# A decoder layer on eight cores: the squares of a 24-tick prologue put last in their ticks, weight loads at other ticks, and eight tile ticks spread over the first own block

## The chip, the cores and the metric

The kernel runs on all 8 cores of one Trainium2 chip, each core on its own 2048 of the 16384 tokens. The metric is device microseconds of the slowest core; the median over runs counts. The engines are PE (TensorE), DVE (VectorE), ACT (ScalarE), POOL (GpSimd) and SP (SyncE, which only issues transfers). Each engine works through its own list of instructions in order, and waits on semaphores.

## What is computed

One decoder layer. The part that matters here is its beginning:

```python
h = rms_norm(x, g_pre_mix[l])
proj = h @ w_in[l]                       # q, k, v (768 each), u (256), gates (2048)
q = apply_rope(q); k = apply_rope(k)
for gi, (window, dilation) in enumerate(((128, 1), (512, 4), (2048, 16))):
    o_g, lse_g = dilated_window_attention(q[group], k[group], v[group], window, dilation)
```

Then the groups are merged by their softmax denominators, a pooling branch and gates are added, an output projection and norm follow, and a SwiGLU FFN with its own norms ends the layer. Since a query looks back up to 2048 tokens, each core also needs k and v of the 2048 tokens ahead of its own, the halo.

## The kernel before

Each core gets its own tokens `xo` (16 tiles of 128 tokens x 1024, f32, 512 KB each) and the halo `xh` (16 tiles, too). Its stages are the halo ticks (to about 82 us), four own blocks of q, k and u projections (to about 210 us), attention (to about 320 us), gates and output projection, and the FFN to the end.

**One tile's way.** SP loads it into `xst` (or, for own tiles 4 to 7, `hTf`). `t_sq` takes its sum of squares on ACT (L394); for halo tiles `rstd_chain` then makes 1/rms in two small POOL instructions (L341, L343), for own tiles ACT takes a root (L400) and `t_rc` a reciprocal on DVE (L404). `t_xs` scales the tile to bf16 in one of three `xsb` buffers, on ACT (L411) for even tiles and on DVE (L413) for odd ones, which frees the load buffer. `t_tr` transposes it on PE in 8 pieces (L424, two PSUM banks in turn), and DVE copies it out with the gain into `hTs` (halo, L432) or `hT` (own). `t_hc` (ACT, L440) keeps 32 columns of each halo tile in `hTc`, for the groups with smaller windows.

**The halo ticks.** Loop over `s_` from 0 to 23. In tick s the tiles s (square), s-2 (scale), s-3 (transpose), s-4 (`t_hc`) and s-8 (`v_stream`: v of group 2, L538) are worked on, and in ticks 7, 8, 11, 12, 15, 16, 19, 20 a `k_stream` (k of group 2 for four tiles: 8 matmuls of 512 columns, L449). Ten buffers hold halo tiles, so tile i+10 is loaded when tile i has been scaled (tick i+2). SP's list is in order: from tick 12 the own tiles 0 to 3 and the tables of cos and sin come in it, at tick 18 the own tiles 4 to 7 and later 8 to 11. In ticks 16 to 22 `own_tick(0)` works on own tiles 0 to 3 in the same stages.

**A rope unit** (`rope_unit`, `rope_flush`): 8 matmuls (L449), an ACT copy to `qb` (L528); then, one unit later, the rotation matmul (L493), two DVE products `t` and `t2b` with the tables (L501, L503) and a POOL addition into `kT` or `qT` (L518). The POOL addition of a unit so stands on POOL in the tick of the flush.

**Weights** come over POOL (`wload`, L74: f32 in memory, cast to bf16 by the transfer). `wplan` says in which tick: `load_wk(g)` and `load_wq(g)` are two transfers of 256 KB (counted as bf16) each, `load_wv(g)` is one of 512 KB. `wk2` and `wv2` are used by the halo ticks (from ticks 7 and 8), the others in the own blocks. `masks` (512 KB) and `wmix` (4 small ones) are first used in attention.

**Own blocks.** Block b has 12 rope units (n = 0 to 11) on own tiles 4b to 4b+3. Block 0 also has, behind n = 3, two halo k units of group 1 (`k_halo`) and four `v_halo`, and behind n = 5 those of group 0. `own_tick(1)` takes the own tiles 4 to 15 through their stages, 8 calls in block 0 and 7 in block 1; `tick_at` says behind which n. Block 1 needs tiles 4 to 7.

## Time and profile before

| | us |
|---|---|
| median of 3 runs | 996.59 |
| lowest run | 996.31 |
| the profiled execution, whole | 1000.57 |
| span of its slowest core (core 7), which all rows below are of | 999.0 |
| spans of the 8 cores | 989.2 to 999.0 |
| PE busy | 926.5 (93%) |
| DVE, ACT, POOL busy | 394.0, 350.3, 320.1 |

The highest of the three runs (1165.07) was a disturbed one and is not used. PE is busy 93% of the span. In forty slices of the page its digit is 9 nearly everywhere but in the first four or five, and there the digit of the DMA engines is 7 to 9. Busy time of PE is modelled at its ends, and in stretches where the granted clock is half, a matmul takes twice as long and still counts as busy.

### The profile page before, as it was taken

The page shows a single profiled execution, that of the slowest core. Times are in us where ns is not written, and L with a number is a line of the kernel's source. Part 1 is how long each engine was busy: PE and PEld are TensorE (multiplying, and loading weights), DVE is VectorE, ACT ScalarE, POOL GpSimd, SP SyncE. Part 2 cuts the span into 40 slices and gives each one's busy share as a digit, 9 for nine tenths or more (in the row PEclk, how much of TensorE's full clock was granted, in tenths as well). Part 3 has the DMA queues.
Part 4 walks back from the last instruction along what each step waited for, and adds up shares of the span by engine and source line. Part 5 has one row for each costly group of instructions (what it writes and reads, how often), then busy time and mean ns, then how long its engine had stood idle before and what let it go on. Part 6 is the DMA issues. An engine that isn't in the chain of part 4 may idle for free.

```text
span 999.0 us, 15229 instructions; the slowest of 8 cores (989.2 to 999.0 us)
## 1 busy us (share of the span) xinstructions
PE 926.5 (93%) x5532; PEld 462.5 (46%) x5532; DVE 394.0 (39%) x552; ACT 350.3 (35%) x603; POOL 320.1 (32%) x318
## 2 busy tenths in 40 slices
PE   1779899998897999999998999999999999999993
PEld 1455454466664444444454444444444444444441
DVE  2576785558876233323677121111112111211111
ACT  4763763369776222224662111110111111111101
POOL 3446587733400433233565111111322000001231
PEclk9999999999998999999999999999999999999997
DMA  8799310000230452114979666664234444430332
GB/s 225 235 231 257 87 47 22 1 2 2 35 53 8 80 84 43 22 22 90 314 252 184 115 110 117 115 108 87 92 127 114 76 85 66 82 64 1 127 110 80
DMA packets 32874, 99.16 MB, mean 99 GB/s; under 512 B 4256, under 2 KB 4256, under 8 KB 32800
## 3 DMA queue, kind: packets, MB, share of 16 engines
q0 software_dynamic: 15296, 42.05, 25.7%
q1 hardware_dynamic: 17360, 56.11, 16.9%
q8 instruction: 45, 0.74, 0.3%
q14 instruction: 29, 0.24, 0.1%
q10 hardware_dynamic: 144, 0.03, 0.0%
HBM read 123.43 MB, written 16.78 MB: 140 GB/s over the span
## 4 chain that ended last, share of the span: by engine, by line
PE 80%; DMA 6%; ACT 4%; issue 4%; DVE 3%; POOL 2%; SPq 1%; DVEq 0%; ACTq 0%; POOLq 0%
PE ps L1229 15%; PE ps L1195 15%; PE ps L1198 15%; PE ps L449 10%; PE ps L969 6%; PE ps L972 6%; PE ps L538 5%; DMA xst<-xh 2%; DMA xin<-xo 2%; DMA xst<-xo 2%; PE ps L979 1%; PE ps L976 1%; PE ps L826 1%; PE ps L804 1%; POOL x1b L1045 1%
## 5 line engine op out<-in xcount | busy, mean ns | idle before, releaser
L1195 PE MATMUL ps<-hT,wgu 128*128 128x512 bf16 x672 | 158.7, 379 | 0.0
L1198 PE MATMUL ps<-hT,wgu 128*128 128x512 bf16 x672 | 158.7, 379 | 0.0
L1229 PE MATMUL ps<-wdn,ffT 128*128 128x512 bf16 x704 | 152.3, 379 | 1.5 <-DMA wdn<-wdn 1.5
L1210 DVE TENSOR_TENSOR ffT<-ps,sa 128x512 bf16<-128x512 f32 x88 | 60.8, 691 | 222.5 <-PE ps L1198 222.5
L1209 ACT ACTIVATE sa<-ps 128x512 f32<-128x512 f32 x88 | 52.7, 598 | 241.5 <-PE ps L1195 241.5
L1229 PEld LDWEIGHTS ps<-wdn,ffT 128*128 128x128 bf16 x704 | 68.8, 98 | 84.7 <-issue 1.9
L1198 PEld LDWEIGHTS ps<-hT,wgu 128*128 128x128 bf16 x672 | 65.7, 98 | 79.3
L1195 PEld LDWEIGHTS ps<-hT,wgu 128*128 128x128 bf16 x672 | 65.6, 98 | 78.6
L74 POOL DMA_DIRECT2D wgu<-wgu x42 | 22.5, 537 | 236.1 <-PE ps L1198 227.5
L449 PE MATMUL ps<-hT,wqk 128*128 128x512 bf16 x384 | 91.6, 383 | 0.6 <-DVE hT L432 0.6
L1045 POOL TENSOR_TENSOR x1b<-tb,xin 128x1024 f32<-128x1024 f32 x31 | 72.8, 2350 | 55.7 <-DVE tb L1040 29.9
L991 POOL TENSOR_TENSOR mT<-m,m 128x512 bf16<-128x512 f32 x32 | 40.5, 1266 | 144.0 <-DVE m L986 144.0
L359 ACT ACTIVATE junk<-ps 128x1024 bf16<-128x1024 f32 x31 | 31.6, 1018 | 139.1 <-PE ps L1229 131.8
L518 POOL TENSOR_TENSOR kT<-t,t2b 128x512 bf16<-128x512 f32 (+1 forms) x36 | 57.5, 1612 | 42.3 <-DVE t2b L503 36.9
L1040 DVE SCALAR_TENSOR_TENSOR tb<-ps,rsA,gfin 128x1024 f32<-128x1024 f32 x15 | 19.3, 1284 | 130.6 <-POOL rsA L343 130.6
L969 PE MATMUL ps<-hT,wgs 128*128 128x512 bf16 x256 | 62.0, 386 | 0.0
L972 PE MATMUL ps<-hT,wgs 128*128 128x512 bf16 x256 | 60.5, 379 | 0.0
L808 ACT ACTIVATE PT<-ps 128x1024 bf16<-128x1024 f32 x48 | 55.4, 1161 | 11.8 <-PE ps L804 11.2
L985 DVE TENSOR_TENSOR m<-ps,sga 128x512 f32<-128x512 f32 x32 | 22.1, 692 | 94.6 <-PE ps L976 91.2
L528 ACT ACTIVATE qb<-ps 128x512 bf16<-128x512 f32 (+1 forms) x60 | 34.9, 584 | 67.8 <-PE ps L449 61.3
L449 PEld LDWEIGHTS ps<-hT,wqk 128*128 128x128 bf16 x384 | 37.3, 99 | 43.6 <-issue 2.5
L1032 PE MATMUL ps<-wout,mT 128*128 128x512 bf16 x256 | 56.9, 379 | 0.0
(131 smaller groups left out, 1175.7 us busy)
## 6 DMA issues: line engine op xcount, KB each, us to landing
wgu<-wgu POOLq DMA_DIRECT2D x42, 512.0 KB, 6.3
xst<-xh SPq DMA_DIRECT2D x16, 512.0 KB, 16.7
xin<-xo SPq DMA_DIRECT2D x16, 512.0 KB, 5.4
x1s<-x1b SPq DMA_DIRECT2D x16, 512.0 KB, 3.7
xin<-x1s SPq DMA_DIRECT2D x16, 512.0 KB, 4.3
out<-x1b SPq DMA_DIRECT2D x15, 512.0 KB, 2.9
xst<-xo SPq DMA_DIRECT2D x12, 512.0 KB, 10.8
wdn<-wdn POOLq DMA_DIRECT2D x22, 256.0 KB, 7.3
```

What stands on the lines that cost most here:

```text
L449: ev = pe.op(lambda e, k=k: e.matmul(ps[:, bank, 0:n], lhsT=wfn(k), rhs=rhsfn(k), start=(k == 0), stop=(k == 7)), signal=(k == 7))
L518: ev_o = pool.op(lambda e: e.tensor_tensor(out=dst, in0=i0, in1=i1, op=ALU.add), waits=[ev_t1, ev_t2])
L808: ev_e = act.op(lambda e: e.activation(out=PT[k3][:, :, :], in_=ps[:, b0:b0 + 2, :], func=AF.Exp, scale=0.125), waits=[ev, pt_free[k3]])
L969: e1 = pe.op(lambda e, k=k, wb=wb, b1=b1, tok=tok: e.matmul(ps[:, b1, :], lhsT=wgs[wb][:, 0, k, :], rhs=hT[:, k, tok], start=(k == 0), sto ...
L972: e2 = pe.op(lambda e, k=k, wb=wb, b2=b2, tok=tok: e.matmul(ps[:, b2, :], lhsT=wgs[wb][:, 1, k, :], rhs=hT[:, k, tok], start=(k == 0), sto ...
L1032: ev = pe.op(lambda e, k=k, hf=hf, pr_=pr_: e.matmul(ps[:, pr_[0] + hf, :], lhsT=mT[:, k, i * 128:(i + 1) * 128], rhs=wout[:, k, hf * 512: ...
L1045: ev_o = pool.op(lambda e: e.tensor_tensor(out=outbuf[:, :], in0=tb[b][:, :], in1=xres[:, :], op=ALU.add), waits=[ev_t, ev_xres, out_free])
L1195: e1 = pe.op(lambda e, k=k, wbuf=wbuf, ba=ba, tok=tok: e.matmul(ps[:, ba, :], lhsT=wbuf[:, 0, k, :], rhs=hT[:, k, tok], start=(k == 0), st ...
L1198: e2 = pe.op(lambda e, k=k, wbuf=wbuf, bb=bb, tok=tok: e.matmul(ps[:, bb, :], lhsT=wbuf[:, 1, k, :], rhs=hT[:, k, tok], start=(k == 0), st ...
L1209: es = act.op(lambda e, ub=ub, ba=ba: e.activation(out=sa[ub][:, :], in_=ps[:, ba, :], func=AF.Silu), waits=[e1, sa_free[ub]])
L1210: ef = dve.op(lambda e, ub=ub, bb=bb, j=j, b=b: e.tensor_tensor(out=ffT[:, j, b * 512:(b + 1) * 512], in0=ps[:, bb, :], in1=sa[ub][:, :], ...
L1229: ev = pe.op(lambda e, j=j, h2=h2, pr_=pr_, il=il: e.matmul(ps[:, pr_[0] + h2, :], lhsT=ffT[:, j, il * 128:(il + 1) * 128], rhs=wdn[:, j, ...
```

## The change

There are four edits. In the halo ticks the square of tile s, with the two POOL instructions behind it, and the weight loads of the tick move from the head of the tick to its end (ahead of `own_tick(0)`). `wplan` has other ticks: wv2 from 1 to 4, wk1 from 11 to 7, wk0 from 13 to 9, wv1 from 15 to 13, wv0 from 17 to 16; the others stay. `masks` and `wmix` are loaded in block 1 behind n = 5 instead of ahead of block 0. In block 0 the eight calls of `own_tick(1)` come behind n = 1, behind each `k_halo(1, ...)`, behind the second and the fourth `v_halo(1, ...)`, and behind n = 5, 7 and 9, instead of behind n = 1, 3, 4, 5, 6, 7, 8, 9.

```diff
-    wplan = {0: [lambda: load_wk(2)], 1: [lambda: load_wv(2)], 2: [lambda: wload("rotm", rotm[:, :], rotm_d[:, :])],
-             11: [lambda: load_wk(1)], 13: [lambda: load_wk(0)], 15: [lambda: load_wv(1)], 17: [lambda: load_wv(0)],
+    wplan = {0: [lambda: load_wk(2)], 4: [lambda: load_wv(2)], 2: [lambda: wload("rotm", rotm[:, :], rotm_d[:, :])],
+             7: [lambda: load_wk(1)], 9: [lambda: load_wk(0)], 13: [lambda: load_wv(1)], 16: [lambda: load_wv(0)],
              19: [lambda: load_wq(2)], 21: [lambda: load_wq(1)], 23: [lambda: load_wq(0)]}
     for s_ in range(NTH + 8):
-        if s_ < NTH:
-            t_sq(s_)
-        for f in wplan.get(s_, ()):
-            f()
         i = s_ - 2
...
             x_load(NTH + s_ - 14)
+        if s_ < NTH:
+            t_sq(s_)
+        for f in wplan.get(s_, ()):
+            f()
         if 16 <= s_ < 23:
             own_tick(0)
...
-    wload("masks", masks[:, :, :], masks_d[:, :, :])
-    for g in range(4):
-        c, hf = g // 2, g % 2
-        wload("wmix", wmixb[64 * hf:64 * hf + 64, c, 64 * hf:64 * hf + 64], wmix_d[g, :, :], waits=[ev_ms4])
     rope_ev = {}
-    tick_at = {0: (1, 3, 4, 5, 6, 7, 8, 9), 1: (0, 2, 4, 6, 8, 9, 10)}
+    tick_at = {0: (1, 5, 7, 9), 1: (0, 2, 4, 6, 8, 9, 10)}
...
                 for pr in range(2):
                     k_halo(1, pr)
+                    own_tick(1)
                 for r in range(4):
                     v_halo(1, r, "dve")
                     if r == 1:
                         rope_flush()
+                    if r % 2:
+                        own_tick(1)
...
             if b == 1 and n == 5:
                 for c2 in range(2):
                     u_halo(c2)
+                wload("masks", masks[:, :, :], masks_d[:, :, :])
+                for g in range(4):
+                    c, hf = g // 2, g % 2
+                    wload("wmix", wmixb[64 * hf:64 * hf + 64, c, 64 * hf:64 * hf + 64], wmix_d[g, :, :], waits=[ev_ms4])
```

SP's list is the same in both kernels. How the others move is seen at three places. First ACT in ticks 5 to 7, as a piece of the difference (`xst_29` holds tile 4, `xst_30` tile 5, `xst_31` tile 6, `xst_32` tile 7; L394 is a square, L411 a scaling, L440 `t_hc`, L528 the copy of the first `k_stream`):

```order
 L394 ACTIVATE junk_39_81,ssA_49<-xst_30_72 128x1024
+L411 ACTIVATE xsb_36_78<-xst_29_71,rsA_51 128x1024
 L440 ACTIVATE hTc_83<-hTs_82 128x8x32
 L394 ACTIVATE junk_38_80,ssA_49<-xst_31_73 128x1024
-L411 ACTIVATE xsb_36_78<-xst_29_71,rsA_51 128x1024
-L440 ACTIVATE hTc_83<-hTs_82 128x8x32
+L440 ACTIVATE hTc_83<-hTs_82 128x8x32
+L528 ACTIVATE qb_52_94<-ps 128x512
 L394 ACTIVATE junk_39_81,ssA_49<-xst_32_74 128x1024
```

The scaling of tile 4 now stands ahead of the square of tile 6, and the copy of the first `k_stream` ahead of the square of tile 7.

Next POOL in ticks 6 to 8, a piece of the difference (L341 and L343 make 1/rms, L518 is the addition of the first `k_stream`):

```order
+L341 TENSOR_SCALAR msA_50<-ssA_49 128x1
+L343 TENSOR_TENSOR rsA_51<-msA_50,nhalf_52 128x1
+L341 TENSOR_SCALAR msA_50<-ssA_49 128x1
+L343 TENSOR_TENSOR rsA_51<-msA_50,nhalf_52 128x1
+L74 DMA wqk_63<-wk 128x1024 x2
 L518 TENSOR_TENSOR kT_16_58<-t_0_54_96,t2b_56_98 128x4x128
 L341 TENSOR_SCALAR msA_50<-ssA_49 128x1
```

The load of wk1 now stands ahead of the first addition, and the pair for tile 8 behind it, where it stood ahead of it before.

Last PE in the halo units of block 0, a piece of the difference (L538 on `hTc` are `v_halo`, L449 on `hT` own units, on `hTd` halo units of group 0, L424 the transposes of own tiles):

```order
 L538 MATMUL ps<-wvr_64,hTc_83 128x256 x16
 L493 MATMUL ps<-qb_53_95,rotm_44 128x512
+L424 MATMUL ps<-ident_43,xsb_37_79 128x128 x8
 L538 MATMUL ps<-wvr_64,hTc_83 128x256 x16
+L424 MATMUL ps<-ident_43,xsb_35_77 128x128 x8
 L449 MATMUL ps<-hT_55,wqk_63 128x512 x16
 L493 MATMUL ps<-qb_52_94,rotm_44 128x512
-L424 MATMUL ps<-ident_43,xsb_37_79 128x128 x8
+L424 MATMUL ps<-ident_43,xsb_36_78 128x128 x8
 L449 MATMUL ps<-hTd_84,wqk_63 128x128 x8
```

Where one own tile had been transposed before the units of group 0, three are now; all of block 0's transposes keep their number, five.

## Rows read from the trace of the kernel before

**Rows 1.** Windows of core 7 by stage; columns as its first line says.
```profile
core 7: us, PE busy (x) PEld busy (x) DVE busy (x) ACT busy (x) POOL busy (x), PEclk, DMA share, GB/s
...
43.00:64.30 21.30, 18.53 (x158) 12.61 (x155) 19.10 (x28) 16.27 (x32) 14.37 (x23) 1.00 0.84 195
64.30:81.70 17.40, 12.56 (x83) 7.99 (x84) 10.48 (x18) 6.63 (x14) 7.54 (x13) 0.80 1.03 256
81.70:101.30 19.60, 19.41 (x110) 10.29 (x111) 10.81 (x21) 8.22 (x15) 11.64 (x8) 1.00 0.96 231
101.30:110.40 9.10, 6.50 (x48) 3.84 (x46) 4.39 (x10) 4.07 (x11) 4.08 (x5) 0.81 0.22 38
110.40:122.60 12.20, 11.58 (x74) 5.65 (x72) 10.42 (x18) 11.83 (x22) 7.56 (x5) 1.00 0.27 68
122.60:149.70 27.10, 27.10 (x182) 14.20 (x181) 23.99 (x39) 17.62 (x31) 22.10 (x13) 1.00 0.23 76
```

**Rows 2.** Windows again, cut by the DMA engines' share (second last column).
```profile
4.00:39.00 35.00, 13.25 (x90) 8.78 (x90) 11.20 (x13) 18.07 (x33) 9.84 (x23) 1.00 0.98 285
39.00:48.00 9.00, 7.86 (x67) 5.32 (x67) 8.06 (x11) 7.21 (x15) 6.95 (x12) 1.00 0.33 102
48.00:99.00 51.00, 43.21 (x301) 26.90 (x300) 35.45 (x57) 25.68 (x51) 29.67 (x33) 0.93 1.02 240
```

**Rows 3.** DMA queues, 0 to 140 us: packets, MB, share of 16 engines.
```profile
q1 hardware_dynamic: 7424, 20.97, 47.4%
q0 software_dynamic: 3200, 5.87, 25.5%
```

**Rows 4.** Timeline, ticks 6 and 7: start, us, instruction, idle before and releaser.
```profile
27.16 1.06 ACT L394 ACTIVATE junk<-xst 128x1024 bf16<-128x1024 f32 x1 [7.64 <-DMA xst<-xh]
28.22 1.14 ACT L411 ACTIVATE xsb<-xst,rsA 128x1024 bf16<-128x1024 f32 x1
...
29.64 1.01 PE L424 MATMUL ps<-ident,xsb 128*128 128x128 bf16 x8 [10.49 <-ACT xsb L411]
30.45 3.62 PE L449 MATMUL ps<-hTs,wqk 128*128 128x512 bf16 x8
```

**Rows 5.** Timeline, ticks 9 and 10: rope products, POOL addition, 1/rms.
```profile
40.97 0.68 DVE L503 TENSOR_TENSOR t2b<-ps,sin 128x512 f32<-128x512 f32 x1
...
41.79 1.27 POOL L518 TENSOR_TENSOR kT<-t,t2b 128x512 bf16<-128x512 f32 x1 [0.70 <-DVE t2b L503]
...
43.15 0.67 POOL L341 TENSOR_SCALAR msA<-ssA 128x1 f32<-128x1 f32 x1
...
43.97 0.55 POOL L343 TENSOR_TENSOR rsA<-msA,nhalf 128x1 f32<-128x1 f32 x1
```

**Rows 6.** Timeline: loads of wk0 and of own tiles 2 and 3 issued.
```profile
51.69 1.16 POOL L74 DMA_DIRECT2D wqk<-wk  x2
53.60 1.50 SPq L74 DMA_DIRECT2D xst<-xo  x2
```

**Rows 7.** Timeline, ticks 19 to 23 and the first own unit.
```profile
64.33 1.89 PE L449 MATMUL ps<-hTs,wqk 128*128 128x512 bf16 x8 [1.50 <-DVE hTs L432]
69.02 1.06 ACT L394 ACTIVATE junk<-xst 128x1024 bf16<-128x1024 f32 x1 [4.71 <-DMA xst<-xo]
72.68 1.06 ACT L394 ACTIVATE junk<-xst 128x1024 bf16<-128x1024 f32 x1 [1.42 <-DMA xst<-xo]
81.68 1.67 PE L449 MATMUL ps<-hT,wqk 128*128 128x512 bf16 x7 [0.60 <-DVE hT L432]
```

**Rows 8.** Timeline, rotation matmuls behind the small halo units of block 0.
```profile
102.86 0.38 PE L493 MATMUL ps<-qb,rotm 128*128 128x512 bf16 x1 [0.87 <-ACT qb L528]
105.40 0.22 PE L493 MATMUL ps<-qb,rotm 128*128 128x128 bf16 x1 [1.72 <-ACT qb L528]
```

**Rows 9.** Timeline, POOL's issues of masks and wmix.
```profile
80.08 0.55 POOL L74 DMA_DIRECT2D masks<-masks  x1
80.60 2.10 POOL L74 DMA_DIRECT2D wmixb<-wmix  x4
```

## What I expect of the change, before seeing it run

> **What bounds the kernel now.** I read the windows by stage first. From 122.6 us on PE is busy without a gap (27.10 of 27.10 us in block 1) [rows 1], so whatever happens earlier is paid or saved once, as the time at which block 1 starts. Before that PE has holes of two kinds: in the halo ticks, and in block 0. The windows cut by the DMA share then say what stands behind the first kind: the 16 DMA engines are full from 4 to 39 us (0.98), nearly empty from 39 to 48 (0.33), and full again from 48 to 99 (1.02) [rows 2]. The timeline shows where fullness hurts: ACT idles 7.64 us for halo tile 6 until 27.16 [rows 4], and 4.71 and 1.42 us for own tiles 2 and 3, until 69.02 and 72.68 [rows 7]. Own tile 2 was issued at 53.60 [rows 6] and so took 15.4 us.
>
> Price of a transfer, from the two queues over 140 us: SP's moved 20.97 MB in 47.4% of the engines (66.4 us, 3.2 us per MB), POOL's 5.87 MB in 25.5% (35.7 us, 6.1 us per MB) [rows 3]. A tile of 0.52 MB so costs all 16 engines 1.7 us, and a weight load (a pair of wk or wq, or one wv, or masks) 3.2 us, since it reads f32.
>
> **1. Squares at the tick's end.** Their number is unchanged; only waits move. In tick 6 ACT waits for tile 6 with the scaling of tile 4 behind it (28.22, 1.14 us); PE gets its transposes at 29.64, after 10.49 idle, and then runs the first `k_stream` at the slow clock, 3.62 us for 8 matmuls [rows 4]. Tile 4 had long landed. In the new order its scaling runs in ACT's gap, at about 19.5 (27.16 less 7.64), its transposes at 21, and the `k_stream` from 21 to 25 (wk2 permitting). Tile 6 itself comes no earlier: wk2, wv2 and rotm still all queue before 27. So at 27.2 the chain is square, copy of the `k_stream`, next square, scaling of tile 6; PE, which had that `k_stream` in front of it until 34.1 (30.45 plus 3.62), does not have it any more. Of the 3.6 us and the 1.1 of the scaling, I count 4.2 as lead at tick 8; bounds 2 (PE has to warm up again after an idle stretch from 25 to 28, and wv2, issued about 5 us later than now, holds the first `v_stream`) and 4.7.
>
> This costs something later. 1/rms of tile s now stands on POOL behind the addition of the same tick. From t2b's end (41.65) addition, L341 and L343 end at 44.52, 2.9 us later [rows 5]. In the fourth tick of each group of four DVE has to scale a tile with just that value, and between t2b and it has only a copy of a transposed tile and a v copy, about 1.6 us. So up to 1.3 us of DVE wait per four ticks, and DVE is the fullest engine there: 19.10 of 21.30 us for eight ticks [rows 1]. That window has 2.2 us of DVE idle, so part of the wait falls into gaps that are there anyway. Three groups of ticks: 0 to 3.9, I take 1.5. The lead at tick 19 is 4.2 - 1.5 = 2.7 us.
>
> **2. Weight loads earlier.** The work of the DMA engines is the same, but 39 to 48 is 67% empty: 6.0 us of engine time [rows 2]. wk1 and wk0 (6.4 us together) move from behind it, wk0 being issued at 51.69 [rows 6], into it or just ahead of it; wv1 comes two ticks earlier, too. What own tiles 2 and 3 queue with: from 48 to 72.7 the engines had own tiles 0 to 3 (6.8 us) and two sets of tables (1.0 MB, 3.4 us), and the other half was POOL's wk1 in part, wk0, wv1, wv0 and wq2. In the new order, from 45 on, the same 10.2 us of SP have wv1 (3.2) and a third of wv0 (1) beside them: 45 + 14.4 = 59.4 us for own tile 3, some 13 us earlier than now. ACT reaches that square in tick 19, at about 64 less the lead, plus 2. So both DMA waits go, and with them the slow clock: the granted clock is 0.80 of full over 64.3 to 81.7 [rows 1], i.e. half of it for 7 us, after PE had idled for the tile.
>
> What is late next there? From 64.33 to 81.68 is 17.35 us [rows 7]. PE is busy 12.56, at most 3.5 of it the half clock's, so 9.1 to 9.8 at full clock; DVE is busy 10.48 [rows 1]. DVE bounds, and the chain root, reciprocal, scaling, transposes, copy of own tile 3 adds about 1.2: 11.7 to 12.5. Saved: 5.0 (bounds 2, if the tiles are late by half of what they are, and 5.8). Block 0 would begin at 81.7 - 2.7 - 5.0 = 74.0.
>
> Beside this stands a rule of the Trainium skill, "DMA: Bandwidth & Descriptors", section "Queues, rings and completion order": each DMA engine takes turns between the queues that have work for it, packet by packet. The stretch 48 to 73, in which POOL's loads and SP's tiles each got about half, agrees. By that rule wk1, issued at about 31 in front of a full line of halo tiles, takes half of the engines from them; it is the second rival below.
>
> **3. Own ticks spread over block 0.** From 81.7 to 122.6, 40.9 us, PE is busy 19.41 + 6.50 + 11.58 = 37.5, of it 1.7 because the clock is 0.81 from 101.3 to 110.4 [rows 1]: 35.8 of dense work, 5.1 lost. The losses stand at one place: ACT idles through the halo units (8.22 of 19.60 busy) and then has two of the moved ticks between the small units, whose rotations PE waits for, 0.87 and 1.72 us [rows 8], upon which the clock falls; afterwards ACT is full, 11.83 of 12.20 [rows 1]. In the new order four of the eight ticks lie in the halo units. A tick costs ACT about 2.4 us (square 1.2, root 0.2, scaling 1.1), each halo unit a copy of 0.6, and PE needs 7.4 us for the six halo calls plus two transposes: ACT 0.6 x 2 + 1.3 + 3 x 2.4 = 9.7 against PE's 8.3. ACT falls behind by about 1.4 and meets the small units with one tick instead of two in front of them. I leave 1.6 us of loss: saved 3.5 (bounds 1.5 and 5.1). Own tile 8 must have landed by 90: what the DMA engines have before it ends about 99 now, and loses wk0, masks and wk1 in part, and starts 3 us earlier, so 87 to 89.
>
> **4. masks and wmix.** 3.2 us less for the DMA engines before 99, counted in 2 and 3. The issues cost POOL 2.65 us [rows 9] behind n = 5 of block 1, where POOL is busy 22.10 of 27.10 and DVE 23.99 [rows 1]. DVE waits for additions two units back, PE for DVE three units on; the 5.0 us of idle POOL time in the block take it in. If the cover were gone it would cost all 2.65; I take 0.5.
>
> **Sum.** 2.7 + 5.0 + 3.5 - 0.5 = 10.7. The profiled execution, 1000.57 whole with a span of 999.0, would have a span of 988.3 and 989.9 whole. The median of the runs is 996.59, 4 us below that execution, and a saving ahead of block 1 moves both alike: 985.9. I round up for the chance that each of the savings meets a new small wait: **986.5**.
>
> **Rivals.** *The forecast*, gain 7 to 13: 0.60. *Less of it*, gain 3 to 6, 992: the lead of tick 8 is eaten by DVE waiting for 1/rms (3.9 instead of 1.5), the slow start of PE, and own tile 8 coming late in block 0. For it speaks that DVE, PE and ACT are all near 10 us per four ticks of 10.65; 0.20. *No change*, within 2 us, 996: the DMA engines bound it all, and what is not waited for at 27, 69 and 72 is waited for elsewhere, since their 0.98 and 1.02 leave nothing. Against it: 6 us are free from 39 to 48, and masks leaves the stretch; 0.08. *More*, gain 14 to 16, 981.5: all upper bounds; 0.07. *Slower*, about 1000: wk1 and wk0 stand in the engines with tiles 10 to 15, which they finish by 39 now [rows 2], and each may come up to 6.4 later. Less the lead that is 2.2 us of PE idle, and a clock that falls once more (7 us at half speed lost 3.5 at 64.3 to 81.7), while own tiles 0 to 3 are issued later by the same amount and the third saving fails by their lateness. It decides if tile 13 lands after 45: tick 13 stands now at 64.3 less one and a half times 10.65, 48.3, and the lead takes off 3. Against it: at 31 the engines have only 8 us of work left; 0.05.
>
> The range that leaves out no more than 2 in 10 goes from 981 (4.7 + 5.8 + 5.1 = 15.6 at best) to 993.5 (a gain of 3). Within 2% means 976.7 to 1016.5, about what a measurement of this kernel can tell from no change: nothing here is worth 20 us, as all of PE's holes before 122.6 that are not the first 14 us come to about that. Faster by over 2%: 0.01; within: 0.97; slower: 0.02.
>
> **What would show it.** Right: the first `k_stream` starts before 25 us; the DMA share of 39 to 48 is above 0.7; no wait of ACT for own tiles above 1 us; no half clock between 64 and 90; the first own unit at 73 to 76; block 1 starts at 111 to 113 and stays dense. Wrong: DVE waiting for rsA in ticks 8 to 15 by more than 2 us in sum; ACT waiting for halo tiles 10 to 15; PE waiting for `qb` in block 0 by more than 2.5 us in sum; POOL's additions late in block 1 so that PE has gaps there.

## The result

The changed kernel takes 989.45 us in the median (988.98 to 991.14); the kernel before, run beside it, 996.85. In some executions of several kernels here one whole die shows a lower granted clock and the time is some per cent longer (one of the six of the kernel before, 1165.07 us); ratios, and all medians and means from here on, leave these out, which makes the kernel before 996.59. The ratio is 0.9931, 95% interval 0.9917 to 0.9944: 7.1 us or 0.7% shorter, where a gain of 10.1 on the median had been forecast. That is inside the forecast range and within 2%.

Page of the changed kernel: span, busy times, clock and DMA shares in 40 slices, and the chain that ended last.

```profile
span 987.7 us, 15224 instructions; the slowest of 8 cores (983.8 to 987.7 us)
...
PE 929.3 (94%) x5532; PEld 463.6 (47%) x5532; DVE 393.6 (40%) x552; ACT 350.0 (35%) x603; POOL 319.3 (32%) x318
...
PEclk9899999999997999999999999999999999999997
DMA  8996420000501641207979767662325435430331
...
PE 89%; DMA 3%; issue 2%; DVE 2%; ACT 2%; POOL 0%; SPq 0%; DVEq 0%; ACTq 0%; POOLq 0%
```

PE now makes 89% of the chain that ended last (80% before), DMA 3% (6% before).

Windows of core 7 of the changed kernel by stage, columns as in [rows 1]. The same eight ticks as in [rows 1] stand at 43.00 to 62.40, what follows them until just behind the first own unit at 62.40 to 76.80, and the end of block 0 with block 1 in the last two rows.

```profile
4.00:39.00 35.00, 18.59 (x124) 11.62 (x125) 15.68 (x19) 21.19 (x38) 13.91 (x29) 0.95 0.99 276
39.00:48.00 9.00, 8.92 (x63) 5.33 (x62) 6.31 (x9) 5.74 (x11) 4.33 (x7) 0.83 1.04 254
48.00:91.00 43.00, 36.86 (x267) 23.15 (x266) 31.97 (x54) 26.45 (x53) 23.89 (x27) 0.96 1.00 255
43.00:62.40 19.40, 15.79 (x137) 10.90 (x135) 16.39 (x24) 16.15 (x33) 10.98 (x16) 1.00 1.01 254
62.40:76.80 14.40, 11.79 (x87) 7.68 (x88) 10.57 (x18) 6.59 (x13) 5.94 (x9) 0.88 1.03 252
...
102.00:112.00 10.00, 10.00 (x61) 5.07 (x59) 7.84 (x13) 7.32 (x13) 7.15 (x6) 1.00 0.56 122
112.00:139.00 27.00, 27.00 (x182) 14.15 (x180) 23.54 (x38) 17.89 (x30) 24.48 (x18) 1.00 0.35 94
```

The hole in the DMA engines' work from 39 to 48 is filled (0.33 in [rows 2], now 1.04). PE has done 18.59 us of work by 39 us, against 13.25. But the granted clock is below 1 where it was full before: 0.95 up to 39 us, 0.83 from 39 to 48.

The timeline of core 7 shows the ticks in which the gain was to arise (start, duration, instruction; in brackets the idle time before it and what ended it).

```profile
18.67 1.13 ACT L411 ACTIVATE xsb<-xst,rsA 128x1024 bf16<-128x1024 f32 x1
...
20.09 1.01 PE L424 MATMUL ps<-ident,xsb 128*128 128x128 bf16 x8 [3.09 <-ACT xsb L411]
21.14 3.57 PE L449 MATMUL ps<-hTs,wqk 128*128 128x512 bf16 x8
...
24.17 1.06 ACT L394 ACTIVATE junk<-xst 128x1024 bf16<-128x1024 f32 x1 [4.06 <-DMA xst<-xh]
...
27.54 1.11 PE L538 MATMUL ps<-wvr,hTs 128*128 128x256 bf16 x8 [2.21 <-DMA wvr<-wv]
28.44 3.54 PE L449 MATMUL ps<-hTs,wqk 128*128 128x512 bf16 x8
```

The scaling of tile 4 and the first `k_stream` now run in the gap, as the forecast had it: 21.14 instead of 30.45 [rows 4]. Two things were not in it. Tile 6 itself came 3 us earlier (24.17, before 27.16), since `wv2` no longer queues ahead of it. In the mean of eight cores its square starts at 23.2 instead of 25.6, and at 25.5 again where `wv2` keeps its old tick (a_squares below). And the second `k_stream` still ran at half clock (3.54 us for eight matmuls that take 1.89 at full clock [rows 7]), behind 2.21 us of PE waiting for `wv2`.

Since one core is not typical of eight here, the stages were averaged over all cores: the start of the last matmul of the last `k_stream` (tick 19), of the first own unit, of the first `u` unit (in block 2), and of the last one, with which the own blocks end, in us. From the last `u` to the end of the span it is 783.5 to 785.7 us in the mean of the cores of every kernel here, so that column decides. All stages come from one execution of each kernel.

| kernel | last `k_stream` | first own unit | first `u` | last `u` | mean span | median of runs |
|---|---|---|---|---|---|---|
| before | 67.2 | 80.7 | 153.8 | 208.2 | 993.9 | 996.59 |
| after | 68.1 | 76.8 | 146.8 | 201.2 | 985.7 | 989.45 |

So the squares' move and the new load ticks together did not shorten the halo ticks at all (67.2 to 68.1). From there to the first own unit it is 8.7 instead of 13.5 us, and from there to the first `u` 70.0 instead of 73.1. Core 7 alone would mislead: on it the last `u` came 9.8 us earlier, 7.0 in the mean.

Where the halo ticks lost their lead is seen in the starts of the eight `k_stream` calls, means of eight cores:

| | 1 | 2 | 3 | 4 | 5 | 6 | 7 | 8 |
|---|---|---|---|---|---|---|---|---|
| before | 28.8 | 33.8 | 41.4 | 44.4 | 52.1 | 55.1 | 62.7 | 65.7 |
| after | 20.6 | 29.4 | 39.5 | 43.0 | 52.3 | 56.0 | 63.6 | 66.6 |

From the second call on a group of four ticks (two calls) took 10.6, 10.7 and 10.6 us before, and 13.6, 13.0 and 10.6 after. The lead was 4.4 us at the second call, 1.4 at the fourth, and gone at the sixth.

Two views of core 7 of the changed kernel say what the groups wait for. First its waits, DVE from 4 to 62 us and then PE from 62 to 112 (us in total, times, longest).

```profile
DVE xsb L413 <- POOL rsA L343: 13.6, 4, 10.1
...
PE ps L424 <- DVE xsb L413: 2.5, 1, 2.5
PE ps L449 <- DVE hTs L432: 1.5, 1, 1.5
PE ps L493 <- ACT qb L528: 1.4, 1, 1.4
```

Beside the one long wait at the start (10.1 us; before 10.3), DVE now waits three times for 1/rms, 3.5 us in sum. From the last `k_stream` to the end of block 0 PE's waits for `qb` fell from 5.0 to 1.4 us.

Then the timeline of one such tick, with POOL, ACT and PE.

```profile
45.40 0.59 ACT L528 ACTIVATE qb<-ps 128x512 bf16<-128x512 f32 x1
45.87 1.06 ACT L394 ACTIVATE junk<-xst 128x1024 bf16<-128x1024 f32 x1
...
46.37 1.65 POOL L518 TENSOR_TENSOR kT<-t,t2b 128x512 bf16<-128x512 f32 x1 [1.44 <-DVE t2b L503]
...
48.10 0.19 POOL L341 TENSOR_SCALAR msA<-ssA 128x1 f32<-128x1 f32 x1
48.44 0.55 POOL L343 TENSOR_TENSOR rsA<-msA,nhalf 128x1 f32<-128x1 f32 x1
...
49.08 1.15 ACT L411 ACTIVATE xsb<-xst,rsA 128x1024 bf16<-128x1024 f32 x1 [0.72 <-POOL rsA L343]
...
50.49 0.61 PE L424 MATMUL ps<-ident,xsb 128*128 128x128 bf16 x8 [1.97 <-ACT xsb L411]
```

1/rms stands behind the addition, the scaling behind 1/rms, and PE idles 1.97 us. The wait for 1/rms is only 0.72 us of this; the square whose 1/rms is waited for also ran late on ACT, behind the copy of the `k_stream`. Here the clock stayed full (the next `k_stream` takes 1.89 us); in other such ticks it falls. Window of core 7 of the changed kernel, right behind a wait of 1.98 us for the same reason:

```profile
39.00:42.00 3.00, 3.00 (x9) 1.04 (x8) 2.03 (x3) 0.00 (x0) 1.97 (x4) 0.50 1.02 319
```

PE is busy all the time and at half speed: the lower level (1.2 GHz) throughout, nine matmuls in 3 us. A `k_stream` there takes 3.58 us. Each core has two such waits of 2.0 us, near 37 and near 50 us, and at 11 of the 16 the clock fell. On core 0 the same happens at 27 to 31 (0.50) and at 49 to 52 us (0.62), while it has full clock from 39 to 42 us.

### The profile page after: what moved, and what is told of

It reads as the page before. It is cut to its first block, busy times and chain, and to the rows that moved or that the text cites. A ratio compares the mean times of both kernels' runs of the same rounds, so it can differ in the third digit from the quotient of the medians.

```text
span 987.7 us, 15224 instructions; the slowest of 8 cores (983.8 to 987.7 us)
## 1 busy us (share of the span) xinstructions
PE 929.3 (94%) x5532; PEld 463.6 (47%) x5532; DVE 393.6 (40%) x552; ACT 350.0 (35%) x603; POOL 319.3 (32%) x318
## 4 chain that ended last, share of the span: by engine, by line
PE 89%; DMA 3%; issue 2%; DVE 2%; ACT 2%; POOL 0%; SPq 0%; DVEq 0%; ACTq 0%; POOLq 0%
PE ps L1232 16%; PE ps L1198 15%; PE ps L1201 15%; PE ps L449 12%; PE ps L972 6%; PE ps L975 6%; PE ps L1035 6%; PE ps L538 5%; PE ps L829 1%; PE ps L982 1%; PE ps L979 1%; PE ps L807 1%; PE ps L493 1%; DMA xst<-xh 1%; DMA wvr<-wv 1%
## 5 line engine op out<-in xcount | busy, mean ns | idle before, releaser
L449 PE MATMUL ps<-hT,wqk 128*128 128x512 bf16 x384 | 90.5, 380 | 0.0
L518 POOL TENSOR_TENSOR kT<-t,t2b 128x512 bf16<-128x512 f32 (+1 forms) x36 | 57.5, 1611 | 38.1 <-DVE t2b L503 25.9
L528 ACT ACTIVATE qb<-ps 128x512 bf16<-128x512 f32 (+1 forms) x60 | 34.9, 583 | 66.0 <-PE ps L449 59.5
L449 PEld LDWEIGHTS ps<-hT,wqk 128*128 128x128 bf16 x384 | 37.1, 98 | 42.6 <-issue 0.5
L811 ACT ACTIVATE PT<-ps 128x1024 bf16<-128x1024 f32 x48 | 52.6, 1095 | 11.8 <-PE ps L807 11.5
```

The costliest lines, as they stand in the source:

```text
L449: ev = pe.op(lambda e, k=k: e.matmul(ps[:, bank, 0:n], lhsT=wfn(k), rhs=rhsfn(k), start=(k == 0), stop=(k == 7)), signal=(k == 7))
L518: ev_o = pool.op(lambda e: e.tensor_tensor(out=dst, in0=i0, in1=i1, op=ALU.add), waits=[ev_t1, ev_t2])
L811: ev_e = act.op(lambda e: e.activation(out=PT[k3][:, :, :], in_=ps[:, b0:b0 + 2, :], func=AF.Exp, scale=0.125), waits=[ev, pt_free[k3]])
```

## The experiments

All times are medians in us, ratios are to the kernel before run beside each, with 95% intervals. Kernels are also called by the first letter of their label. "Last `u`" is the mean over eight cores of one execution, as above (before 208.2, after 201.2). How far one execution can be trusted is seen where two kernels share their code: before, c_masks and d_spread agree within 0.1 us up to the last `k_stream`, while a_squares and f_no_wplan differ there by 0.7, and h_middle and n_mid_wv_late by 0.6 at the fourth `k_stream`, before their difference begins. The table at the end of this section has the mean span over all executions of each kernel.

### Each part alone

**The squares and loads at the tick's end, with the tick numbers of before.**

```diff
-        if s_ < NTH: t_sq(s_); then wplan      # at the head
+        if s_ < NTH: t_sq(s_); then wplan      # behind x_load
```

> Only the first edit: squares, their 1/rms pair and the loads of a tick at the tick's end, with the old ticks of the loads. The theory of the prediction (lead at tick 8 of about 4, of which 1.5 is lost until tick 19, nothing gained where own tiles are late, because wk0, wv1 and wv0 still stand ahead of them): the first own unit starts 1 to 2.7 us earlier than before on the mean core, and the run is 0.5 to 2.5 us shorter. Rival (the edit carries the whole gain of the full change): first own unit 5 us earlier, 6 to 7 us shorter. Rival (the edit costs more in the steady ticks than it brings, since 1/rms waits behind the POOL addition): the first own unit is not earlier.

Measured: 993.28, ratio 0.9961 (0.9948 to 0.9974); last `u` 202.2. The second `k_stream` started at 25.6 instead of 33.8, the last was 4.4 us earlier, not 8, and the groups of four took 13.1, 12.0 and 10.6 us. So the first two groups eat half of the lead with the loads at their old ticks, too. All the same the theory was too low: the first own unit came 6.2 us earlier in the mean (74.5), not 1 to 2.7, and the run gained 3.9 by the ratio, not 0.5 to 2.5. Of the 6.2 us 4.4 are from the halo ticks and 1.8 from behind them, where ACT's wait for own tiles fell from 6.9 to 4.2 us. This is also, with f_no_wplan below, the kernel whose cores differ most. The calls L449 on own tiles, first on core 0, then on core 1 (durations, first and last start):

```profile
L449 PE MATMUL ps<-hT,wqk x384: 376/379/634, 78.6 to 204.7; 128*128 128x512 bf16 x192
```
```profile
L449 PE MATMUL ps<-hT,wqk x384: 376/379/635, 71.2 to 197.6; 128*128 128x512 bf16 x192
```

Two neighbouring cores with the same program are 7 us apart. ACT waits for own tiles by 9.6, 9.0, 8.8 and 5.8 us on cores 0, 2, 4 and 6, and not at all on cores 1, 3, 5 and 7. The slowest core sets the time, so 6.0 us at the last `u` of the mean core became only those 3.9.

**The tick numbers alone, at the head.**

```diff
-1: load_wv(2), 11: load_wk(1), 13: load_wk(0), 15: load_wv(1), 17: load_wv(0)
+4: load_wv(2),  7: load_wk(1),  9: load_wk(0), 13: load_wv(1), 16: load_wv(0)
```

> Only the second edit: the weight loads at their new ticks, but at the head of the tick. Theory: ACT's wait for own tile 2 (4.7 us) falls under 1 us, no half clock between 64 and 80 us, first own unit 3 to 4.5 us earlier on the mean core, run 3 to 4.5 us shorter. It also tells whether wv2 at tick 4 lets halo tile 6 land 3 us earlier (its square at 24.2 instead of 27.2), as in the full change, or whether that came from elsewhere. Rival (the engines' total work bounds, a hole filled is a hole elsewhere): no change within 1 us.

Measured: 992.6, 0.9960 (0.9944 to 0.9976); last `u` 204.7. The first `k_stream` starts at 26.7 instead of 28.8 and all later ones keep 1.8 to 2.2 us of it: tile 6 lands earlier (its square starts at 23.4 instead of 25.6) because `wv2` does not stand before it. From the last `k_stream` to the first own unit it is 11.6 instead of 13.5. That is the whole gain of the filled hole when it stands alone: ACT still waits 3.8 us for own tile 2, where under 1 had been expected.

**masks and wmix alone.**

```diff
-    wload("masks", ...); 4 x wload("wmix", ...)   # ahead of block 0
+    wload("masks", ...); 4 x wload("wmix", ...)   # behind u_halo, block 1, n = 5
```

> Only the third edit: masks and wmix loaded in block 1. Theory: they are issued behind everything block 0 needs, so only own tiles 8 to 11 can gain; less than 1 us either way, and block 1 stays dense. Rival: own tile 8 lands late now and its waiting goes, 1 to 3 us shorter. Rival: POOL's 2.65 us of issuing in block 1 shows, 0.5 to 2.7 us longer.

Measured: 997.36, 1.0010 (0.9996 to 1.0025); last `u` 207.8, mean span over nine executions 992.4 against 992.2. Neither a gain nor a cost is shown.

**The spread of own ticks alone.**

```diff
-    tick_at = {0: (1, 3, 4, 5, 6, 7, 8, 9), ...
+    tick_at = {0: (1, 5, 7, 9), ...     # and own_tick(1) four times in the halo units at n == 3
```

> Only the fourth edit: the eight own ticks of block 0 in the halo units. Theory: the waits of PE for qb behind the small halo units (0.87 and 1.72 us) and the fall of the clock behind them shrink: block 0 takes 2.5 to 4 us less, run 2.5 to 4 us shorter. Rival: with the tiles no earlier than before, own tile 8 (landed near 99 us) is late for its square, now called at about 97: ACT stands in front of it and PE waits for qb, so the gain is under 1 us alone and needs the other edits.

Measured: 993.37, 0.9963 (0.9945 to 0.9981); last `u` 204.1. From the first own unit to the first `u` it is 69.6 instead of 73.1: 3.5 us, the term of the forecast.

The parts alone give 6.0, 3.5, 0.4 and 4.1, in sum 14.0 us at the last `u`; together they give 7.0. By the mean spans over all executions they are 5.6, 3.7, -0.3 and 3.7, in sum 12.6 before rounding, and 6.9 together, so the loss is not one of a single execution. The first two take from each other, and they do it in the halo ticks: alone they bring the last `k_stream` 4.4 and 1.8 us forward, together they put it 0.9 back.

### The change without one part, or with one step placed otherwise

**Without the squares' move** (b, c and d together).

```diff
+        if s_ < NTH: t_sq(s_); then wplan      # back at the head
-        if s_ < NTH: t_sq(s_); then wplan
```

> The full change without moving the squares (new ticks of the loads at the head of the tick, masks late, own ticks spread). If these three add up: 208.2 - 3.5 - 0.4 - 4.1 = 200.2 for the end of the own blocks on the mean core, that is no later than the full change with its 201.2, and a run of the same time. Then the squares' move brings nothing beside the others.

Measured: 990.14, 0.9933 (0.9912 to 0.9955); last `u` 201.1, after has 201.2. Groups of four: 10.6, 10.8, 10.6. Beside the other parts the move of the squares to this place brings nothing.

**Without the new tick numbers** (a, c and d together).

```diff
+1: load_wv(2), 11: load_wk(1), 13: load_wk(0), 15: load_wv(1), 17: load_wv(0)
```

> The full change without the new ticks of the weight loads (squares last, masks late, own ticks spread). If the parts added up, the end of the own blocks would stand at 208.2 - 6.0 - 0.4 - 4.1 = 197.7 on the mean core, against 201.2 for the full change: the new ticks would then cost 3.5 us beside the other edits though they gain 3.5 alone. Rival (the parts overlap whatever they are, since own tiles come no sooner): 200 to 202.

Measured: 989.38, 0.9922 (0.9903 to 0.9941); last `u` 199.4, in the mean 1.8 us earlier than with them, between the sum of the parts (197.7) and the rival's 200 to 202. The last `k_stream` stands at 63.5, 4.6 us before that of the changed kernel. The median is that of the changed kernel all the same: the cores' last `u` stands between 195.3 and 204.8 here, and the cores' spans differ by 10 to 11 us in each of the four executions, against 4 to 9 in the changed kernel. The new numbers cost the halo ticks and bring the cores together.

**`wv2` back at tick 1, else the changed kernel.**

```diff
-    wplan = {0: ..., 4: [lambda: load_wv(2)], 2: ...
+    wplan = {0: ..., 1: [lambda: load_wv(2)], 2: ...
```

> The full change with wv2 back in tick 1 (at its end). Theory A (the late wv2 is what spoils the halo ticks: PE waits 2 to 4 us for it in front of the first v_stream, the second k_stream runs late and at half clock): that wait goes, the second k_stream starts at about 26 on the mean core instead of 29, the last at 64 to 66 instead of 68.1, first own unit at 74 to 75 instead of 76.8, run 1.5 to 3 us shorter than the full change. Theory B (wk1 and wk0, put in front of halo tiles, spoil them): squares of tiles 7 to 12 stay late, the last k_stream stays within 1 us of 68, and the run within 1 us.

Measured: 988.63, 0.9921 (0.9899 to 0.9942); last `u` 199.5. The second `k_stream` starts at 26.5 instead of 29.4: PE's wait for `wv2` and the half clock behind it had cost 2.9 us there. But the next two groups take 14.0 and 12.8, the last `k_stream` is 2.7 us earlier, and 1.7 us are left at the last `u` (0.8 in the median).

**The square in the middle of the tick**: directly behind the copy `t_hc`, ahead of the v and k streams, so that 1/rms stands ahead of the addition on POOL, and on ACT the square ahead of the tick's copies of v and k but still behind the scaling. The loads stay at the end.

```diff
             t_hc(s_ - 4)
+        if s_ < NTH:
+            t_sq(s_)
...
-        if s_ < NTH:
-            t_sq(s_)
```

> The full change, but the square of a tick behind t_hc and ahead of v_stream and k_stream, so that scaling of tile s-2 still comes ahead of it, and its 1/rms pair stands ahead of the POOL addition of the tick. Theory (1/rms behind the addition makes DVE and ACT wait, about 1 us in every four ticks): PE's waits for xsb of about 2.0 us at 37 and 50 go, groups of four ticks take 10.7 us instead of 11.5, first own unit 2 to 3 us earlier than the full change. Rival: the copy of the first k_stream now stands behind a square that waits for a halo tile, and gives the same back: within 1 us.

Measured: 987.44, 0.9905 (0.9888 to 0.9923); last `u` 198.3, 2.9 us earlier than after. The groups take 11.9, 10.6 and 10.6. In its timeline (core 6, same tick as above) 1/rms now stands ahead of the addition (spans on POOL are rough; the two overlap as drawn), ACT scales the tile without a wait, and PE idles 0.21 us instead of 1.97:

```profile
41.79 1.09 POOL L343 TENSOR_TENSOR rsA<-msA,nhalf 128x1 f32<-128x1 f32 x1
...
42.32 1.64 POOL L518 TENSOR_TENSOR kT<-t,t2b 128x512 bf16<-128x512 f32 x1
...
43.28 1.14 ACT L411 ACTIVATE xsb<-xst,rsA 128x1024 bf16<-128x1024 f32 x1
...
44.67 0.61 PE L424 MATMUL ps<-ident,xsb 128*128 128x128 bf16 x8 [0.21 <-ACT xsb L411]
```

One line in another place removes the price of the move: in the second group 2.4 us against the changed kernel, with everything else equal. The line changes the order on two engines at once, on POOL (1/rms and addition) and on ACT (square and copy of the `k_stream`); how much is due to which was not tried.

### Putting the two findings together

**The middle, and `wv2` at tick 1.**

```diff
-    wplan = {0: ..., 4: [lambda: load_wv(2)], 2: ...    # in the kernel with the middle
+    wplan = {0: ..., 1: [lambda: load_wv(2)], 2: ...
```

> The full change with the square behind t_hc and wv2 back in tick 1, both. Alone against the full change, these brought the end of the own blocks on the mean core from 201.2 to 198.3 and to 199.5. If they are two causes, they add up: about 196.6, run about 985.5. Rival (one cause, the fall of the clock after PE idles in the halo ticks, which either of them mends): no better than 198, run about 987.5.

Measured: 990.7, 0.9938 (0.9921 to 0.9954); last `u` 201.6. That is a clear miss: the last `k_stream` came 1.4 us earlier than with the middle alone, and the first own unit 3.4 us later. ACT waited 8.8 us for own tiles, means of eight cores (middle alone 4.0, after 0.0, before 6.9).

**The squares at the end up to tick 7, at the head from tick 8 on**, with `wv2` at tick 1.

```diff
+        if 8 <= s_ < NTH: t_sq(s_)     # head
+        if s_ < 8: t_sq(s_)            # end
```

> wv2 in tick 1, squares last in ticks 0 to 7 only, and at the head of the tick from tick 8 on, as before the change; the rest as in the full change. Theory (what eats the lead is the square at the end of the steady ticks, whose 1/rms comes behind the addition): the second k_stream starts at about 25.5 as in i_wv2_tick1, but groups of four ticks take 10.7 us from there instead of 14.0 and 11.5; last k_stream at 60 to 62.5 instead of 65.4. Rival (the lead is lost whatever the order, since the halo tiles land only so fast): last k_stream at 63 to 65.

Measured: 987.49, 0.9905 (0.9888 to 0.9923); last `u` 199.5. The groups take 15.0, 10.8 and 10.6, and the last `k_stream` stands at 63.5, which is in the rival's range (63 to 65) and not in the theory's. So from the second group on the price is gone with the squares back at the head, as with the middle. The first group is long here and with the middle and `wv2` at tick 1 (13.5), once the second `k_stream` stands at 25.6. Core 0 of this kernel, the window of 25 to 38 us and the square of tile 6:

```profile
25.00:38.00 13.00, 8.76 (x57) 6.12 (x57) 7.42 (x11) 11.33 (x22) 8.23 (x15) 0.74 1.01 315
```
```profile
25.44 1.06 ACT L394 ACTIVATE junk<-xst 128x1024 bf16<-128x1024 f32 x1 [6.25 <-DMA xst<-xh]
```

ACT idles 6.25 us until tile 6 lands and is then busy 11.33 of 13.00 us; the only wait for a tile in that window after it is 0.20 us. What follows the second `k_stream` hangs on the tiles from 6 on, and their work starts when tile 6 is there, however early the calls before it ran. A lead at the second `k_stream` is therefore in part no lead. The clock is at its lower level for half of the window (0.74), too.

**As j, with wk1 and wk0 two ticks later**, so that the halo tiles 10 to 15 have less beside them.

```diff
-    7: [lambda: load_wk(1)], 9: [lambda: load_wk(0)]
+    9: [lambda: load_wk(1)], 11: [lambda: load_wk(0)]
```

> As j_mid_wv2, but wk1 in tick 9 and wk0 in tick 11 instead of 7 and 9. Theory (in ticks 7 and 9 they take the engines from halo tiles 10 to 15 that ACT then waits for): last k_stream 0.5 to 1.5 us earlier than in j_mid_wv2, own tiles 2 and 3 waited for by up to 2 us on some cores; in sum within 1 us. Rival (the tiles do not wait for the engines at that time): last k_stream the same, own tiles later, first own unit 0.5 to 2 us later.

Measured: 993.04, 0.9954 (0.9938 to 0.9969), with much spread among its runs (989.66 to 994.59); last `u` 200.9 in the profiled execution, which is one of the shortest: its mean span is 984.4, that of all eight 986.5. The last `k_stream` is another 0.6 us earlier (61.7) and ACT waits 8.3 us for own tiles. The halo end is not the bound any more; the own tiles are.

**The middle, with wv1 and wv0 late.**

```diff
-    13: [lambda: load_wv(1)], 16: [lambda: load_wv(0)]    # in the kernel with the middle
+    18: [lambda: load_wv(1)], 20: [lambda: load_wv(0)]
```

> As h_middle, but wv1 in tick 18 and wv0 in tick 20 instead of 13 and 16. In h_middle ACT still waits 4.0 us for own tiles 2 and 3 (mean core) with the engines full. Theory (wv1 and wv0 take the engines from own tiles 0 to 3, which need to land by tick 19): those waits fall to 0 to 1 us, first own unit 2 to 3 us earlier than in h_middle (74.3 there), i.e. 71.5 to 72.5, unless wv1 and wv0 then come late for block 0 (they are used at about 85 and 96); run about 985.5. Rival (own tiles land late because SP's own queue is slow or because all 8 cores share the memory, whatever POOL's loads do): waits 3 to 4 us as in h_middle, first own unit 74 to 75, run 987 to 988.

Measured: **984.94** (984.38 to 985.58), 0.9876 (0.9854 to 0.9898); last `u` 195.8. It is 11.7 us ahead of the kernel before and 4.5 ahead of the changed one. ACT's wait for own tiles is 0.2 us (h_middle 4.0), the first own unit starts at 71.7 (74.4). Own tile 2 takes 10.1 us from issue to landing in the mean of eight cores, in h_middle, which differs in nothing but these two loads, 13.4.

It shows most on core 0 of j_mid_wv2 and of this kernel, which also differ in the tick of `wv2`. First j_mid_wv2: own tile 2 issued, the load of `wv1` beside it, and the square that waits.

```profile
47.28 1.37 SPq L74 DMA_DIRECT2D xst<-xo  x2
...
47.45 0.73 POOL L74 DMA_DIRECT2D wvr<-wv  x1
...
66.50 1.06 ACT L394 ACTIVATE junk<-xst 128x1024 bf16<-128x1024 f32 x1 [6.28 <-DMA xst<-xo]
```

Then the kernel with `wv1` late:

```profile
47.01 1.47 SPq L74 DMA_DIRECT2D xst<-xo  x2
...
57.62 0.62 POOL L74 DMA_DIRECT2D wvr<-wv  x1
...
58.67 1.06 ACT L394 ACTIVATE junk<-xst 128x1024 bf16<-128x1024 f32 x1 [1.09 <-DMA xst<-xo]
```

Issued at the same time, the tile is there after 11.7 us instead of 19.2, once POOL's queue holds nothing new beside it. On core 0 of h_middle, where `wv1` is at its earlier tick and `wv2` as here, it lands after 12.0, so on this core `wv1` alone does not make the difference; the tick of `wv2`, with which all issues of the stretch move, has a part. The engines are full in both cases (share 1.00 and 0.99 from 50 to 60 us); in those 10 us they moved 262 GB/s in the one and 316 in the other. The DMA queues from 50 to 60 us, first j_mid_wv2 and then this kernel (packets, MB, share of 16 engines; q1 is SP's, q0 POOL's):

```profile
q1 hardware_dynamic: 853, 2.07, 68.5%
q0 software_dynamic: 146, 0.53, 30.6%
```
```profile
q1 hardware_dynamic: 1310, 3.15, 98.6%
```

So the full engines did half as much again of the tiles' work.

**The mean span over all executions.** Mean over the eight cores, then over the executions of each kernel, in us. For the kernel before they are those run beside the single edits.

| kernel | executions | mean span | lowest to highest |
|---|---|---|---|
| before | 12 | 992.2 | 991.2 to 992.6 |
| after | 6 | 985.3 | 984.8 to 985.7 |
| a_squares | 5 | 986.6 | 986.3 to 986.9 |
| b_wplan | 4 | 988.4 | 988.1 to 989.1 |
| c_masks | 9 | 992.4 | 991.9 to 993.5 |
| d_spread | 4 | 988.5 | 987.8 to 988.8 |
| e_no_squares | 4 | 985.1 | 984.6 to 985.5 |
| f_no_wplan | 4 | 982.7 | 982.1 to 983.3 |
| i_wv2_tick1 | 3 | 983.2 | 982.8 to 983.7 |
| h_middle | 4 | 982.7 | 982.1 to 983.6 |
| j_mid_wv2 | 5 | 986.3 | 986.1 to 986.6 |
| k_last_to_7 | 6 | 983.1 | 982.0 to 984.4 |
| l_mid_wk_9_11 | 8 | 986.5 | 984.4 to 988.3 |
| n_mid_wv_late | 4 | 980.8 | 980.6 to 981.1 |

Less the last `u` they come to 783.3 to 785.0 us in every kernel but l_mid_wk_9_11, whose profiled execution was one of its shortest. That of the kernel before was a long one (mean span 993.9), and most of its excess lies behind the last `u`.

## Why the prediction was right, and where it was not

The number came within 3 us, by a sum of which one term failed, one held, and one held in number for a reason that was not in the forecast (means of eight cores; forecast, measured). The range it had to hit, gains of 3 to 15.6 us, was wide.

| term | forecast | measured |
|---|---|---|
| lead at tick 19 | 2.7 | -0.9 |
| own tiles 0 to 3 | 5.0 | 4.8 |
| block 0, less POOL's issues in block 1 | 3.0 | 3.1 |
| sum at the last `u` | 10.7 | 7.0 |

**Squares at the tick's end: wrong in size, and the sign of what is left.** The forecast counted 4.2 us of lead at tick 8; 4.4 were there at the second `k_stream`. That was luck: the move alone gives 8.2 there (a_squares), and the late `wv2` takes 2.9 of it back (i_wv2_tick1). "Three groups of ticks: 0 to 3.9, I take 1.5" is the step that failed: the three groups lost 5.3 us. The mechanism named was a true one (1/rms behind the addition). DVE's waits for it came to 3.5 us on core 7, near the upper bound and above the 2 us that the forecast itself called a sign of being wrong; the forecast let them fall into gaps of DVE that were there anyway. It also left out three things: ACT scales such tiles too (1.5 us of waits of its own in 30 to 62 us); the square of such a tick stands behind the copy of the `k_stream` on ACT; and PE idles about 2 us each time, upon which the clock went to half level in one or two groups, at 1.7 us per `k_stream`. h_middle against the changed kernel puts the price of the order in the second group at 2.4 us, i against k (same load ticks) at 2.0. In the first group the order costs 1.7 us (after 13.6, h 11.9), while k and j, both with an earlier second `k_stream`, have 15.0 and 13.5: there the landing of tile 6 at about 25, ACT's work behind it and the half clock take their part. How much is due to which was not separated.

**The clash with the load ticks was not in the forecast.** With the old ticks the same squares bring the last `k_stream` forward by 4.4 us (a_squares; f_no_wplan 3.7), more than the 2.7 forecast; with the new ones it is 0.9 late. Of the 4.6 us between f_no_wplan and the changed kernel, `wv2` at tick 4 makes 2.7 (i_wv2_tick1) and the four other loads together the remaining 1.9. With the squares at the head of the tick the new ticks cost nothing there: PE does not wait for `wv2` in b_wplan and e_no_squares at all, and by 1.9 to 4.0 us on each core of the changed kernel, because only the moved squares let PE come to the first `v_stream` before `wv2` has landed.

**`wv2` at tick 4.** The forecast had it as a bound only ("wv2, issued about 5 us later than now, holds the first `v_stream`"). It held it on every core: PE waited 1.9 to 4.0 us (core 7: 2.21), and i_wv2_tick1 shows 2.9 us at the second `k_stream`. "Tile 6 itself comes no earlier" was wrong: b_wplan, in which `wv2` is the only load that moved before tick 7, has the first `k_stream` 2.1 us earlier. In the changed kernel the late `wv2` costs more than it brings, 1.7 us at the last `u` (i_wv2_tick1); in the kernel with the middle it is the other way round, by 3.3 (j_mid_wv2), because of the own tiles.

**Weight loads earlier: right in number, in part by luck.** The share of 39 to 48 went from 0.33 to 1.04, ACT's wait for own tiles from 6.9 to 0.0, and the way from the last `k_stream` to the first own unit from 13.5 to 8.7. The half clock, forecast to be gone between 64 and 90, went away by half: 0.80 over 17.4 us is 7 us at the lower level, 0.88 over 14.4 is 3.5, around a wait of PE of 2.48 us for the scaling of an own tile. Window and timeline of core 7 of the changed kernel:

```profile
72.00:75.00 3.00, 1.82 (x13) 1.57 (x14) 2.07 (x4) 0.00 (x0) 2.74 (x5) 0.62 0.99 264
```
```profile
73.18 1.01 PE L424 MATMUL ps<-ident,xsb 128*128 128x128 bf16 x8 [2.48 <-DVE xsb L413]
73.98 1.91 PE L538 MATMUL ps<-wvr,hTs 128*128 128x256 bf16 x8
```

Part of the 4.8 us is owed to the first term's failure: with ticks 8 to 19 not ahead, own tiles had that much longer to land. The new ticks alone give only 1.9 here (b_wplan), and with the halo ticks ahead, as the forecast had them, 2.8 (h_middle). Where the halo ticks are 4 to 6 us shorter than in the changed kernel (h, j, k, l), ACT waits 4.0 to 8.8 us again. n_mid_wv_late, which gives the tiles the engines, collects both.

**The rule of turn-taking by queue** stood in the forecast beside the rival that ends slower (it is called the second there and stands last): wk1 and wk0 in the way of halo tiles 10 to 15. That did not come: ACT waits for no halo tile from 30 to 62 us on any core of the changed kernel. For the own tiles h_middle and n_mid_wv_late show the price of two loads beside them, 4.0 against 0.2 us of ACT's waiting. The Trainium skill, "DMA: Bandwidth & Descriptors", section "Queues, rings and completion order", has each DMA engine take turns between the queues with work. The queue rows above agree in that both are served at once, 68.5% and 30.6% of the engines' time; what the share would be by that rule no run here shows. Nor is the load beside a tile the whole of it. In a_squares `wk0` is issued 1.2 us behind own tile 2 on core 0 and 0.4 us behind it on core 1, and the tile takes 19.1 us on the one and 9.4 on the other. And own tile 2 takes 18.1 us in j and 10.0 in the changed kernel (means of eight cores), where `wv1` came 1 us behind it (50.88 behind 49.76 on core 0); on that core all loads from `wk0` on are issued earlier in j, and yet fewer bytes are moved by 70 us (17.7 MB, 18.3 in the changed kernel). That stays open.

**Spread: right.** 3.5 us alone (d_spread), 3.1 in the changed kernel; PE's waits for `qb` 1.4 us on core 7, none of them with a lower clock behind it. **masks and wmix: right** in that nothing is lost that shows, and block 1 stays dense (27.00 of 27.00). Block 1 began at 112.8 on core 7 (122.6 less the 9.8 by which its first `u` is earlier), forecast 111 to 113, the first own unit at 75.7, forecast 74.0.

**The rivals.** The gain, 7.1 by the medians, lies just inside the forecast's 7 to 13 and above *Less of it* (3 to 6), but two of the three causes named for the latter came true: DVE's waits for 1/rms near 3.9 us, and PE's slow start. *No change* fell with the ratio (0.9917 to 0.9944); *More* with the first term.

**What core 7 hid.** The sum was worked out on the slowest core of one execution. On that core it was nearly right (9.8 for 10.7), and the rest of the difference between the two spans (11.3 us) lies behind the own blocks, where nothing was changed. The mean over the cores gained 7.0. The hole in the DMA engines' work, too, was deepest on core 7: from 39 to 48 us the share is 0.33 there, and 0.36 to 0.74 on the other cores of the same execution, 0.53 in the mean of all eight. So the forecast's 6.0 us of free engine time are 4.2 on the mean core. (In the forecast's own working, 17.35 less 11.7 gives 5.7 as the upper bound of the second term, not 5.8.)

## What to carry to other kernels

Where a small operation that others wait for (here 1/rms, 0.7 us) moves to the end of a tick, ask on each in-order queue what it now stands behind; the square belonged neither at the head of the tick (the scaling behind the late tile) nor at its end (1/rms behind the addition, the square behind the copy) but between them. With full DMA engines, filling the hole earlier shortened the way to the first own unit by 1.9 us alone, and keeping the other queue empty while the tiles fly on which the path waits brought another 2.5. Read every stage on all cores before a sum is made: parts that save time on the same path must be tested together, as 14 us of single gains were 7 in company, and 12 when the square and two loads had found other places.

## What the runs showed of the hardware

- With full DMA engines a 0.52 MB tile took from 6.8 to 20.4 us to land (own tile 2, cores of a_squares and j_mid_wv2). Moving two loads of the other queue away changed the mean from 13.4 to 10.1 us (h_middle, n_mid_wv_late). With the same loads, neighbouring cores differed by more: 19.1 and 9.4, 18.4 and 10.3, 17.7 and 6.8, 15.3 and 9.8 us on the four pairs of a_squares, and the first two then stood 7 us apart (78.6 and 71.2).
- Full DMA engines moved between 232 GB/s (j_mid_wv2, core 0, 60 to 70 us, share 1.04) and 334 (after, core 3, 27 to 31 us, share 1.00); the full share did not tell the rate.
- At 11 of 16 waits of PE of 2.0 us in the halo ticks of the changed kernel the granted clock went to its lower level (1.2 GHz) in the following 3 to 4 us (0.50 from 39 to 42 us on core 7, though PE was busy for 3.00 of 3.00): 3.58 us instead of 1.89 for eight matmuls. On other cores the same tick stayed at full clock, and on core 7 the next such wait (50.49) was followed by full clock.
